# Hybrid sublayer: gate products in front of the squares, scores of attention step 6 in front of tile 0's output transposes

## The reference

```python
def hybrid_mixer(h, pos, w_in, w_out, sink, lb, norm_w):
    aq, ak, av, bq, bff, bfb, bi, bg = jnp.split(h @ w_in, offs, axis=-1)
    o_a = window_attention(aq, ak, av, pos, sink)          # 8 heads, softmax with a sink column
    o_b = hgrn2_bidir(bq, bff, bfb, bi, bg, lb, norm_w)    # 4 heads, both directions
    return jnp.concatenate([o_a, o_b], axis=-1) @ w_out
# end of hgrn2_bidir:
    o = rms_norm(o, norm_w[:, None, :])
    return o * jax.nn.silu(hg)
```

## Time and profile before

| | us |
|---|---|
| median of 3 runs | 1080.91 (1080.79 to 1081.02) |
| the profiled execution | 1080.24 |
| its span, first to last instruction | 1078.5 |
| PE busy | 1008.2 |
| DVE busy | 803.1 |
| ACT busy | 493.8 |
| POOL busy | 71.5 |

### The profile page before, as it was taken

How to read it: one execution, slowest core, us unless ns; L and a number is a source line. 1 busy time by engine, 2 the same in 40 slices (tenths; PEclk the granted TensorE clock), 3 DMA queues, 4 the chain that set the end, 5 groups by cost and what they waited for, 6 DMA issues and landing times.

```text
span 1078.5 us, 13123 instructions
## 1 busy us (share of the span) xinstructions
PE 1008.2 (93%) x5004; PEld 837.6 (78%) x5004; DVE 803.1 (74%) x1147; ACT 493.8 (46%) x713; POOL 71.5 (7%) x172
## 2 busy tenths in 40 slices
PE   1799999999998999999999999999898989999996
PEld 1588888879976788888887888888677777888885
DVE  5898888877787787888778788787656577666465
ACT  2443434356866454344445434344465554434340
POOL 0000000001310000000000000000521000000000
PEclk9899999999999999999999999999899999999998
DMA  9999999636233499879758988961233339466531
GB/s 362 387 376 379 327 366 373 242 108 231 83 113 127 140 361 361 311 288 338 261 197 323 319 299 289 396 217 35 88 113 97 115 127 355 165 224 219 202 117 40
DMA packets 72463, 255.32 MB, mean 237 GB/s; under 512 B 8784, under 2 KB 10064, under 8 KB 72400
## 3 DMA queue, kind: packets, MB, share of 16 engines
q1 hardware_dynamic: 69088, 243.43, 62.8%
q0 software_dynamic: 3168, 10.52, 3.0%
q10 hardware_dynamic: 144, 0.52, 0.1%
HBM read 253.37 MB, written 1.07 MB: 236 GB/s over the span
## 4 chain that ended last, share of the span: by engine, by line
PE 77%; DVE 9%; issue 4%; ACT 4%; POOL 2%; DMA 2%; DVEq 0%; SPq 0%; ACTq 0%; POOLq 0%
PE bank L1503 24%; PE bank L1507 24%; PE bank L1506 24%; DVE w_lo L962 3%; PE bank L1838 2%; DMA w_raw<-in_w_dram 2%; ACT w_hi L701 1%; DVE arena L970 1%; PE bank L1609 1%; PE bank L1632 1%; PE bank L1599 1%; PE bank L1498 1%; POOL arena L659 1%; PE bank L1714 1%; ACT arena L728 0%
## 5 line engine op out<-in xcount | busy, mean ns | idle before, releaser
L962 DVE TENSOR_TENSOR w_lo<-w_raw,w_hi 128x2048 fp32r<-128x2048 f32 (+2 forms) x164 | 360.0, 2216 | 47.0 <-ACT w_hi L701 47.0
L1503 PE MATMUL bank<-w_hi,hT_hi 128*128 128x512 f32 (+3 forms) x880 | 352.0, 400 | 27.3 <-DVE w_lo L962 14.4
L1507 PE MATMUL bank<-w_lo,hT_hi 128*128 128x512 f32 (+3 forms) x880 | 342.0, 389 | 0.0
L1506 PE MATMUL bank<-w_hi,hT_lo 128*128 128x512 f32 (+3 forms) x880 | 341.5, 388 | 0.0
L701 ACT ACTIVATE w_hi<-w_raw 128x2048 fp32r<-128x2048 f32 (+2 forms) x164 | 303.7, 1856 | 41.6 <-DMA w_raw<-in_w_dram 34.2
L1503 PEld LDWEIGHTS bank<-w_hi,hT_hi 128*128 128x128 f32 x880 | 167.8, 191 | 59.7 <-issue 18.2
L1507 PEld LDWEIGHTS bank<-w_lo,hT_hi 128*128 128x128 f32 x880 | 167.5, 190 | 34.1
L1506 PEld LDWEIGHTS bank<-w_hi,hT_lo 128*128 128x128 f32 x880 | 168.0, 191 | 29.9
L970 DVE SCALAR_TENSOR_TENSOR arena<-arena,c_row 128x1024 f32<-128x1024 f32 x144 | 171.0, 1218 | 10.2 <-DMA arena<-in_ada_w_dram 10.0
L763 ACT ACTIVATE arena<-bank 128x256 f32<-128x256 f32 x88 | 33.7, 383 | 305.1 <-PE bank L1507 305.1
L1503 PE MATMUL bank<-w_hi,fT_hi 128*128 128x512 f32 x352 | 137.8, 391 | 1.3 <-DVE fT_lo L1438 1.3
(11 more groups left out here) (212 smaller groups left out, 810.1 us busy)
## 6 DMA issues: line engine op xcount, KB each, us to landing
w_raw<-in_w_dram SPq DMA_DIRECT2D x310, 512.0 KB, 5.6
arena<-in_ada_w_dram SPq DMA_DIRECT2D x144, 512.0 KB, 7.2
gate_row<-gate_scratch POOLq DMA_DIRECT2D x6, 512.0 KB, 5.0
arena<-in_ln_g_dram POOLq DMA_DIRECT2D x6, 512.0 KB, 5.1
arena<-in_ln_b_dram POOLq DMA_DIRECT2D x6, 512.0 KB, 6.8
w_raw<-in_w_dram SPq DMA_DIRECT2D x8, 256.0 KB, 2.9
w_raw<-in_w_dram SPq DMA_DIRECT2D x8, 192.0 KB, 2.9
x<-in_x_dram ACTq DMA_DIRECT2D x1, 512.0 KB, 5.7
```

The source lines that it names most:

```text
L962: nc.vector.tensor_tensor(w_lo[:, j0 % RING, 0:n], w_raw[:, j0 % RAW, 0:n], w_hi[:, j0 % RING, 0:n].bitcast(F32), ALU.subtract)\
L1503: mm = nc.tensor.matmul(dst, a_hi, b_hi, start=start, stop=False)
L1506: nc.tensor.matmul(dst, a_lo, b_hi, start=False, stop=False)
L1507: return nc.tensor.matmul(dst, a_hi, b_lo, start=False, stop=stop)
```

## The change

One place of `hybrid_plan()` is written in another order. `gate` moves from behind `lo` 15 to the place right behind `O` 7, before the two `sq`. `attention_step(6, 8)`, which is S 6, P 5, V 4, is taken apart: S 6 is put in front of `owin` 0, and P 5 and V 4 stay behind it. Nothing is added or left out, and no semaphore changes.

```diff
@@ -333,9 +333,8 @@
             yield from (("lo", 14), ("A", 7), ("O", 6), ("M", 7), ("hi", 15))
             yield from attention_step(5, 8)
-            yield from (("O", 7), ("sq", 0), ("sq", 1), ("owin", 0))
-            yield from attention_step(6, 8)
-            yield from (("lo", 15), ("gate", 0), ("out", (0, 0)), ("hi", 16))
+            yield from (("O", 7), ("gate", 0), ("sq", 0), ("sq", 1), ("S", 6), ("owin", 0), ("P", 5), ("V", 4))
+            yield from (("lo", 15), ("out", (0, 0)), ("hi", 16))
             yield from attention_step(7, 8)
```

## The result

The changed kernel takes 1085.07 us (median of 6 runs, 1083.09 to 1086.33), the kernel before 1080.85 us in the same comparison (6 runs, 1080.19 to 1081.02). The ratio is 1.0041, with a 95% interval of 1.003 to 1.0052: slower by about 4.2 us. The forecast was 1085.2, range 1082.7 to 1087.6.

What follows compares the result with a forecast made beforehand. PE, busy 93% of the span, was taken to bound the kernel, though led by other engines in this stretch. Queue 2.67, clock 1.6 and gate 0 make 4.3 us over 1080.91: 1085.2 us, range 1082.7 to 1087.6.

Steps and rivals of the forecast that it cites:

- The queue: On ACT and DVE, owin 0's parts stand behind S 6's maximum and exponents; out (0, 0) starts 2.67 us late.
- The cost is on ACT: Owin 0's high part on ACT would stand behind S 6's exponents, running from 337.14 instead of 332.81.
- The rival in which the change pays: S 6's maximum is ready by 333, so DVE starts S 7 1.2 us sooner: 1079.7 us, chance 0.03.
- The clock: After PE's long idle time, a 3.4 us half-clock spell slows 8 products of out (0, 0): 1.6 us.
- The gate: Gate products move into DVE's idle time before the squares' sums; worth 0, bounded by 1.2 us of gain.
- both waits end together at S 7: Before S 7, DVE's gate products end at 339.57 and PE's scores at 339.47; removing DVE's wait alone gains nothing.
- SP and lo 15: Late lo 15 delays SP's load of slot 18 to about 346.4, ahead of its use; no cost.
- Sum: Whole kernel: 2.67 + 1.6 + 0 = 4.3 us slower, median 1085.2 us.
- the clock's rivals: Two cases of slow spells falling otherwise: one more (1086.2 to 1087.6 us, 0.14) or one vanishing (1081.2 to 1082.8, 0.11).
- a spell more: A further slow spell after a short wait later on, or all 12 products slow: another 1 to 2.4 us, chance 0.14.
- time given back later: A spell of before, such as the one at 834, may vanish, giving back 2.4 us: 1082.8 us, chance 0.11.
- the sign that the sublayer ends about 4 us later and the rest keeps the distance: Sublayer's last product ends about 4 us later than before, and the rest of the program keeps that distance.

Runs made afterwards that it cites:

- e2: Kernel before with only S 6 moved in front of owin 0, on all engines, gate products left behind lo 15: 1085.09 us, ratio 1.004 to before.
- e3: Kernel before with gate products ahead of the squares and S 6 ahead of owin 0 on PE alone: 1080.16 us, ratio 0.9992 to before.
- e7: Changed kernel, but ACT makes owin 0's high part ahead of S 6's exponents: 1082.05 us, ratio 1.0008 to before.
- e5: Changed kernel, but POOL makes the sink copy of S 6 ahead of its two powers: 1083.66 us, ratio 1.0027 to before.
- e6: Changed kernel, but ACT makes owin 0's high part ahead of S 6's exponents and the squares stand behind lo 15: 1080.36 us, ratio 0.999 to before.
- e4: Changed kernel with 20 extra matmuls on PE between V 4 and out (0, 0), so PE does not idle there: 1084.69 us, ratio 1.003 to before.
- e9: Kernel before with 7 extra matmuls on PE between O 7 and owin 0, so PE is not idle there: 1080.58 us, ratio 0.9989 to before.
- g_again: A second trace of the kernel before with only the gate products moved in front of the squares: 1080.17 us.
- e1: Kernel before with only the gate products moved in front of the squares, owin 0 still ahead of S 6: 1080.38 us, ratio 0.9999 to before.
- a_again: The changed kernel, unchanged, for one more trace: 1085.18 us.
- b_again: The kernel before, unchanged, for one more trace: 1080.60 us.

## Why the prediction was right

- *The queue (2.67 us)*: measured 2.70 in both traces of the changed kernel. The links came as listed: sink copy, maximum, exponents, high part, low part, out (0, 0). e2, e3 and e7 show that it is ACT's and DVE's lists, e5 that POOL sets the maximum. "The cost is on ACT" was half of it: with ACT's list put back, e7 still has DVE's low part behind the maximum, and DVE alone makes 2.20 of the 3.94 us against e3. The rival in which the change pays asked for the maximum to be ready early; e6 makes it so (it starts 4.6 us behind S 5 instead of 8.3), with ACT's high part first as well, and out (0, 0) comes at 6.77.
- *The clock (1.6 us)*: 1.84 measured, of which e4 takes away 1.81. The mechanism was right and the spell mis-sized: I took 3.4 us beginning as work restarts, it was 6.8 us, of which the last 3.9 met work. That the errors nearly cancel is luck. The idle time was 4.86 us, not 4.2. That the 1.84 us are in the kernel's time is argued from the sum; e4 did not show it in the medians.
- *The gate (0)*: right in the changed kernel, where DVE then waits 3.35 us for PE. The reason given, that both waits end together at S 7, is shown by e9 and g_again. e1 shows the condition that I named (PE must come sooner) met by the clock alone: then it is worth 1.24 us up to S 7, which its median does not show.
- *SP and lo 15*: no trace of a wait for a weight slot in the stretch; 0 was right.
- *Sum*: 4.54 us locally against 4.3, 4.2 in the medians. That the medians fit so well is partly luck: the traced run held both of the clock's rivals at once, a spell more (from 5.07 at 356.12 to 6.66 at 371.85) and time given back later (to 5.0 at the end). The spell more came behind a wait of 1.3 us ahead of the sublayer's last transposes, as that rival had it, and came again in a_again. So the sign that the sublayer ends about 4 us later and the rest keeps the distance failed: it ended 6.1 us later and the rest did not keep it.

## What to carry to other kernels

A plan that all engines walk ties moves together that should be judged engine by engine: look for what each engine's list puts behind the moved step's longest wait. Here a stage was moved forward on the engine that had time for it and dragged its waits in front of finished work on two others; ordering each engine for itself, and moving what had slack behind, turned a loss of 4 us into a gain of 1.8 (0.6 to 3.0). Where two waits end together, price each with the other gone before calling it free.

## What the runs showed of the hardware

Slow spells of TensorE came at different places in runs of one unchanged kernel. The gate-only kernel took 1076.62 us at a mean granted clock of 0.989 and 1085.89 us at 0.979; the kernel before 1078.68 us at 0.986 and 1085.26 us at 0.979. So runs of one kernel lay 6 to 9 us apart, more than any edit here moved them, and the slowest of these had the lowest clock. It is not always so: the slowest run of e5, 1086.69 us, had 0.986, its set's fastest, 1081.62 us, 0.984. So spells are not the whole of the spread, and what else is in it stays open. After the same 1.80 us of idle time the clock fell in the traces of before, b_again and g_again (from 331 to 332 on) and stayed full in e1; where S 6 cut it to 1.17 us, it stayed full at that place in all nine traces. The wait of 1.33 us ahead of owin 1's transposes is the same in all fourteen traces: a slow spell began within 1 us of its end in five (both of the changed kernel, e2, e3 and e5) and not in the other nine. By these traces neither the length of a wait nor the kernel alone says whether a spell follows.
